# Attention rounds of a two-block transformer: all score products of a round at its head, in five banks, with the preceding pair's values behind them

## The chip, the cores and the metric

One Trainium2 chip, of which the program uses one core. The metric is device microseconds of one launch of the whole program, from inputs in HBM to the output in HBM. Engines are named as in the profile: PE is TensorE (the matrix engine), PEld its weight loads, DVE VectorE, ACT ScalarE, POOL GpSimd, SP the engine that issues most transfers. A bank is one of the eight PSUM banks of 128 x 512 f32, here G0, G1, S0, S1, T0, T1, O0 and O1 (bank0 to bank7).

## What is computed

Two transformer blocks on 512 tokens of width 1024, all in f32. The first has two kinds of attention, the second a gated linear attention and a dilated one:

```
block 1:  q,k,v of 8 MoBA heads (64 wide)  -> softmax(q k^T + bias) v        4 pairs of heads
          q1,q2,k1,k2,v of 4 diff heads    -> (softmax(q1 k1^T + bias)
                                             - lam * softmax(q2 k2^T + bias)) v, RMS norm   4 heads
          merged = sigmoid(ga) * (ya @ w_a) + sigmoid(gb) * (yb @ w_b);  x += norm(merged @ w_out)
          x += norm((silu(h @ w_gate) * (h @ w_up)) @ w_down)
block 2:  gated linear attention (4 heads) and dilated attention (8 heads = 4 pairs) side by side,
          then w_out, a causal convolution between w_up and the gating, w_down
```

All attention is causal. So of the 4 x 4 tiles of 128 queries by 128 keys, rows r = 0 to 3 have 1 to 4 tiles: 128, 256, 384 and 512 keys.

## The kernel before

Large products are made of f32r parts: each weight tile is split into w_hi and w_lo (ACT rounds, DVE subtracts, L1252 and L1833), each activation likewise, and one step is three matmuls of 128 x 512 (hi*hi, hi*lo, lo*hi). Everything inside attention (scores, transposes, values) is plain f32.

Attention goes in 12 rounds, i = 0 to 11, each with one pair: rounds 0 to 3 a pair of MoBA heads, 4 to 7 the two maps of one diff head, 8 to 11 a pair of dilated heads. All loops are unrolled, and each engine runs its own list in the order in which the code is written; semaphores are all that ties them. In a round PE has a filler, the projection or output steps of the next pair (32, 40 or 24 steps of three matmuls; `fill`, `dilated_fill`), and the attention work is put between the steps of the filler at the step numbers in the tables TURNS, LAST_TURNS (round 7) and DILATED_TURNS.

For pair i the work on PE is:

- `pair_scores(i, r)` (L858): for each of the two maps m, qT[64 rows of map m, 128 queries of row r] against k[64 rows, 128(r+1) keys]. Map 0 uses partitions 0 to 63 and bank S0, map 1 partitions 64 to 127 and bank S1: each is a 64 x 128 part of the array. In the trace one f32 matmul leaves two records.
- `turn(i, n)` (L877): transposes of the probabilities, n = 0 for rows 0 and 1, n = 1 for row 2, n = 2 for row 3, into banks T0 (map 0) and T1 (map 1; not used in rounds 4 to 7, where the maps have been joined).
- `pair_values(i)` (L895 and L898), a round later: values times transposed probabilities into O0. With two maps each is a 128 x 64 part of the array (L895), in rounds 4 to 7 it is the whole array (L898).
- `pair_squares` (L906) and, in the dilated rounds, `turn_dilated_values` (L1165) and `dilated_norm_sums` (L1172), which use bank O1.

In between, DVE reads the scores with the bias added (`pair_logits`, L1995, signals `sc_read`), ACT takes the exponential (`exps`, L1358), DVE and ACT scale by the row sum (`scale_rows` L2003 and L2007, `scale_other` L1366, `join_rows` L2017; signals `w_ready`, `w_other`), and after each turn DVE and ACT copy the transposed rows to SBUF (`store_turned`, L2027 to L2031, L1374 to L1378; signals `turned0`, `turned1`).

S0 and S1 hold rows 0 and 1 side by side, then row 2, then row 3, each written when the row before has been read. A round goes so on PE: scores of rows 0 and 1, filler, values of the preceding pair, scores of row 2, filler, turn 0, filler, scores of row 3, filler, turn 1, filler, turn 2, filler.

Of the kernel before, what the change touches and what calls it, by code (L numbers as in the profile page):

```python
# [26 lines left out]
P = 128  # L27
S = 512
# [64 lines left out]
TURNS = {4: (5, 9, 9, 13, 17, 23), 5: (5, 9, 9, 15, 21, 28)}  # L93
LAST_TURNS = (5, 9, 9, 12, 15, 20)
# [4 lines left out]
DILATED_TURNS = {24: (2, 5, 9, 11, 11, 15, 19, 20), 21: (1, 4, 8, 8, 9, 13, 13, 18)}  # L99
# [3 lines left out]
def two_maps(i):  # L103

    return i < 4 or i >= 8
# [79 lines left out]
def build(nc, a, out):  # L185
    with ExitStack() as ctx:
# [274 lines left out]
        def scores_at(r):  # L461

            return P if r == 1 else 0
# [153 lines left out]
        def _(pe):  # L617
# [230 lines left out]
            def pair_scores(i, r):  # L848

                n, at_ = P * (r + 1), scores_at(r)  # L850
                qk_ = qk if i < 8 else qk_dil
                for m in range(2):
                    if r == 0 and i >= 1:
                        pe.wait_ge(sc_read, 8 * i - 1 + m)
                    if r >= 2:
                        pe.wait_ge(sc_read, 8 * i + 2 * r - 1 + m)
                    h = slice(64 * m, 64 * m + 64)
                    ins = pe.matmul(SB_[m][:, at_:at_ + n], qk_[h, i % 2, 0, P * r:P * r + P], qk_[h, i % 2, 1, 0:n],  # L858
                                    start=True, stop=True)
                    if r >= 1:  # L860
                        ins.then_inc(sc_ready, 1)

            def turn(i, n):
# [4 lines left out]
                pe.wait_ge(w_ready, 4 * i + rows[-1] + 1)  # L868
                pe.wait_ge(turned0, 3 * i + n) if i or n else None
# [32 lines left out]
            def pair_squares(i):  # L902

                pe.wait_ge(o_sq, i - 3)
                pe.wait_ge(o_rs, i - 4) if i >= 5 else None
                pe.matmul(O1[:, :], ones[:, :], sqacc[:, :], start=True, stop=True).then_inc(o_ms, 1)  # L906

            for i in range(8):
                steps = KU * len(ROUNDS[i][1])
                values, scores2, turn0, scores3, turn1, turn2 = LAST_TURNS if i == 7 else TURNS[len(ROUNDS[i][1])]  # L910
# [18 lines left out]
                pair_scores(i, 3)  # L929
                fill(i, scores3, turn1)  # L930
# [229 lines left out]
            def turn_dilated_values(p):  # L1160

                pe.wait_ge(v_staged, p + 1)
                pe.wait_ge(qk_rs[1], p + 1)
                for j in range(NT):
# [1548 lines left out]
```

## Time and profile before

| | |
|---|---|
| median of 3 runs | 1394.62 us (1394.3 to 1395.87) |
| profiled execution, first to last instruction (span) | 1394.0 us |
| PE busy | 1375.2 us (99%), 6662 matmul records |
| PEld busy | 1105.7 us (79%) |
| DVE busy | 875.7 us (63%) |
| ACT busy | 584.4 us (42%) |
| rounds 0 to 7 | about 65 to 318 us of the span |
| rounds 8 to 11 | about 894 to 997 us |

The profiled execution has no time of its own beside its span; the three timed runs, which hold what lies before the first and after the last instruction, are 0.3 to 1.9 us above the span. A busy engine in this profile is one with an instruction under way. Records of matmuls overlap, since each lasts until its last result is written; how fast PE advances is read from the distance between the starts of matmuls.

### The profile page before, as it was taken

To read this page: it belongs to the slowest core of one execution; us is meant where nothing else is said; L and a number is where in the kernel's file an instruction comes from. 1 tells how busy PE (TensorE), PEld (TensorE's weight loads), DVE (VectorE), ACT (ScalarE), POOL (GpSimd) and SP (SyncE) were. 2 spreads that over 40 slices of the span, in tenths; PEclk is the share of its full clock that TensorE was granted. 3 is DMA by queue.
4 is the path that set the end of the run, shared out by engine and by line. 5 is a ranking of instruction groups with operands and counts; after the bars stand their busy time and mean duration, and the time that the engine had idled before them with its cause. 6 is when DMAs were issued, how large, how long until landed. Compare 5 with 4: busy or idle time off the path is not lost.

```text
span 1394.0 us, 18973 instructions
## 1 busy us (share of the span) xinstructions
PE 1375.2 (99%) x6662; PEld 1105.7 (79%) x6662; DVE 875.7 (63%) x1473; ACT 584.4 (42%) x979; POOL 57.4 (4%) x119
## 2 busy tenths in 40 slices
PE   9999999999999999999998999999999999999999
PEld 7777777778988888888885787777798888888887
DVE  6666666678777777774336777766566665665221
ACT  5444545553453323223224534666445444443221
POOL 0000000000001211211000000000000000000000
PEclk9999999999999999999999999999999999999999
DMA  5222122213225555554431221111212322223332
GB/s 205 92 75 76 67 70 76 76 61 121 91 73 190 197 190 190 192 194 153 141 124 47 96 68 61 62 61 62 72 61 92 104 90 101 94 93 116 93 98 87
DMA packets 42614, 146.82 MB, mean 105 GB/s; under 512 B 5424, under 2 KB 5696, under 8 KB 42560
## 3 DMA queue, kind: packets, MB, share of 16 engines
q1 hardware_dynamic: 34592, 120.13, 26.1%
q0 software_dynamic: 7824, 25.70, 5.4%
q8 instruction: 35, 0.57, 0.2%
q10 hardware_dynamic: 144, 0.26, 0.1%
q14 instruction: 19, 0.16, 0.0%
HBM read 143.97 MB, written 2.10 MB: 105 GB/s over the span
## 4 chain that ended last, share of the span: by engine, by line
PE 93%; DVE 4%; ACT 2%; issue 1%; DMA 0%; SPq 0%; DVEq 0%; ACTq 0%
PE bank L634 62%; PE bank L836 13%; PE bank L652 4%; PE bank L775 3%; PE bank L858 2%; PE bank L877 2%; PE bank L950 2%; PE bank L895 1%; PE bank L742 1%; PE bank L1080 1%; PE bank L898 1%; DVE w_lo L1833 1%; DVE gate_a L2040 0%; DVE hbuf L1893 0%; PE bank L1172 0%
## 5 line engine op out<-in xcount | busy, mean ns | idle before, releaser
L1833 DVE TENSOR_TENSOR w_lo<-raw,w_hi 128x1024 fp32r<-128x1024 f32 (+1 forms) x224 | 268.0, 1197 | 160.8 <-ACT w_hi L1252 155.9
L1252 ACT ACTIVATE w_hi<-raw 128x1024 fp32r<-128x1024 f32 (+1 forms) x224 | 231.6, 1035 | 285.9 <-PE bank L634 260.7
L634 PE MATMUL bank<-h_hi,w_hi 128*128 128x512 f32 x856 | 339.5, 397 | 0.7 <-DVE w_lo L1830 0.5
L634 PE MATMUL bank<-h_hi,w_lo 128*128 128x512 f32 x856 | 334.1, 390 | 0.0
L634 PE MATMUL bank<-h_lo,w_hi 128*128 128x512 f32 x856 | 334.0, 390 | 0.0
L634 PEld LDWEIGHTS bank<-h_hi,w_hi 128*128 128x128 f32 x856 | 161.0, 188 | 41.2 <-issue 7.4
L634 PEld LDWEIGHTS bank<-h_hi,w_lo 128*128 128x128 f32 x856 | 161.1, 188 | 33.9
L634 PEld LDWEIGHTS bank<-h_lo,w_hi 128*128 128x128 f32 x856 | 161.1, 188 | 33.3 <-issue 1.0
L634 PE MATMUL bank<-f_hi,w_lo 128*128 128x512 f32 x352 | 136.9, 389 | 0.0
L634 PE MATMUL bank<-f_hi,w_hi 128*128 128x512 f32 x352 | 136.9, 389 | 0.0
L634 PE MATMUL bank<-f_lo,w_hi 128*128 128x512 f32 x352 | 136.9, 389 | 0.0
L836 PE MATMUL bank<-h_hi,w_hi 128*128 128x512 f32 x240 | 98.4, 410 | 0.4 <-DVE ma L2046 0.4
L836 PE MATMUL bank<-h_hi,w_lo 128*128 128x512 f32 x240 | 93.9, 391 | 0.0
L836 PE MATMUL bank<-h_lo,w_hi 128*128 128x512 f32 x240 | 93.6, 390 | 0.0
L634 PEld LDWEIGHTS bank<-f_hi,w_hi 128*128 128x128 f32 x352 | 66.1, 188 | 13.8
L634 PEld LDWEIGHTS bank<-f_hi,w_lo 128*128 128x128 f32 x352 | 66.1, 188 | 13.6
L634 PEld LDWEIGHTS bank<-f_lo,w_hi 128*128 128x128 f32 x352 | 66.1, 188 | 13.6
L2258 DVE CUSTOM_DVE_ANT_0 ada<-ada,cond 128x512 f32<-128x512 f32 x96 | 63.5, 689 | 16.5 <-DMA ada<-in_w_ada 15.0
L520 POOL DMA_DIRECT2D ada<-in_w_ada x96 | 51.5, 536 | 364.8 <-DVE ada_sum L2258 358.8
L836 PEld LDWEIGHTS bank<-h_hi,w_hi 128*128 128x128 f32 x240 | 45.1, 188 | 21.4 <-issue 13.6
L2244 DVE TENSOR_TENSOR f_lo<-fbuf,f_hi 128x512 f32 (+1 forms) x44 | 30.5, 692 | 43.0 <-ACT f_hi L1794 21.5
L836 PEld LDWEIGHTS bank<-h_hi,w_lo 128*128 128x128 f32 x240 | 45.0, 188 | 10.1
(351 smaller groups left out, 1954.3 us busy)
## 6 DMA issues: line engine op xcount, KB each, us to landing
raw<-in_w_up SPq DMA_DIRECT2D x66, 512.0 KB, 3.3
ada<-in_w_ada POOLq DMA_DIRECT2D x96, 256.0 KB, 3.1
raw<-in_w_mix SPq DMA_DIRECT2D x47, 512.0 KB, 3.3
raw<-in_w_down SPq DMA_DIRECT2D x32, 512.0 KB, 3.5
raw<-in_w_in SPq DMA_DIRECT2D x25, 512.0 KB, 3.3
raw<-in_w_gate SPq DMA_DIRECT2D x22, 512.0 KB, 3.2
raw<-in_w_out SPq DMA_DIRECT2D x16, 512.0 KB, 3.3
raw<-in_w_down SPq DMA_DIRECT2D x16, 384.0 KB, 3.3
```

Source lines behind the costliest of these rows:

```text
L520: pool.dma_start(ada[:, half, :], a["w_ada"][bass.ds(t, 1), :, half * S:half * S + S] .rearrange("t p k -> (t p) k")).then_inc(ada_in[half ...
L634: last = pe.matmul(to[:, :], wt[:, slot, k, :], act_[:, rhs0 + k, :], start=(k == first and n == 0), stop=(k == K - 1 and n == 2))
L652: last = pe.matmul(to[:, TOKENS[h]], wt[:, slot, k, :], act_[:, k, TOKENS[h]], start=(k == 0 and m == 0), stop=(k == KU - 1 and m == 2))
L775: last = pe.matmul(banks[r][:, :], xt[:, k, P * r:P * r + P], wt[:, slot, 4 * kk:4 * kk + 4, :].rearrange("p a b -> p (a b)"), start=(k == ...
L836: last = pe.matmul(output_bank(u)[:, :], wt[:, slot, k, :], act_[:, kr, :], start=(kr == 0 and m == 0), stop=(kr == length - 1 and m == 2))
L858: ins = pe.matmul(SB_[m][:, at_:at_ + n], qk_[h, i % 2, 0, P * r:P * r + P], qk_[h, i % 2, 1, 0:n], start=True, stop=True)
L877: last = pe.transpose(TB[m][:, at_:at_ + P], probs_[:, m, ROWOFF[r] + P * j:ROWOFF[r] + P * j + P], ident[:, :])
L950: last = pe.matmul(output_bank(u)[:, :], wt[:, slot, 4 * half + k, :], act_[:, 4 + k, :], start=(k == 0 and m == 0), stop=(k == 3 and m == 2))
L1252: act.activation(w_hi[:, s, k0:K, :], raw[:, s, k0:K, :], ACT.Copy).then_inc(hi_ready[s], 1)
L1833: dve.tensor_tensor(w_lo[:, s, k0:K, :], raw[:, s, k0:K, :], w_hi[:, s, k0:K, :].bitcast(F32), ALU.subtract).then_inc(split_ready[s], 1)
L2244: dve.tensor_tensor(at_k(f_lo, j), fbuf[:, :], at_k(f_hi, j).bitcast(F32), ALU.subtract).then_inc(f_ready, 1)
L2258: dve.tensor_tensor_reduce(ada[:, half, :], ada[:, half, :], cond[:, half * S:half * S + S], 1.0, 0.0, ALU.mult, ALU.add, ada_sum[:, parit ...
```

## The change

- `pair_scores(i)` now issues all eight matmuls of the pair at the head of the round, in the order SCORES (map, row): (0,0), (1,0), (0,2), (1,2), (0,1), (1,3), (0,3), (1,1). They go to five banks: row 3 to S0 and S1, rows 0 and 2 side by side to T0 (map 0) and T1 (map 1), row 1 of both maps side by side to O1. Before (1,1) it waits until (0,1) is done, which is in the same bank. Five of the matmuls signal instead of six.
- `pair_values(i - 1)` follows straight behind, before the first filler step.
- Ahead of the scores are new waits: all turned rows of the preceding pair stored, all its scores read; in rounds 6 and 7 O1 read by the norm; in round 8 `gy_f32`, which was ahead of turn 0. Turn 0, the squares and the turned dilated values wait for the reads of T0, T1 and O1.
- DVE reads the rows in the order 0, 2, 1, 3, the first three at the head of the round. Row 3 keeps its place.
- The tables lose the entries for scores and values. The turned dilated values go from step 2 to 4 (in round 11 from 1 to 3); all turns, squares and norm sums keep their step numbers.

```diff
-TURNS = {4: (5, 9, 9, 13, 17, 23), 5: (5, 9, 9, 15, 21, 28)}
-LAST_TURNS = (5, 9, 9, 12, 15, 20)
+TURNS = {4: (9, 9, 17, 23), 5: (9, 9, 21, 28)}
+LAST_TURNS = (9, 9, 15, 20)
+SCORES = ((0, 0), (1, 0), (0, 2), (1, 2), (0, 1), (1, 3), (0, 3), (1, 1))
+SCORED = ((0, 2), (1, 2), (0, 1), (0, 3), (1, 1))
+READABLE = {(0, 0): 1, (0, 2): 1, (1, 0): 2, (1, 2): 2, (0, 1): 5, (1, 1): 5, (0, 3): 5, (1, 3): 5}
+READ_ORDER = (0, 2, 1, 3)
-DILATED_TURNS = {24: (2, 5, 9, 11, 11, 15, 19, 20), 21: (1, 4, 8, 8, 9, 13, 13, 18)}
+DILATED_TURNS = {24: (4, 9, 11, 15, 19, 20), 21: (3, 8, 8, 13, 13, 18)}
...
-        def scores_at(r):
-
-            return P if r == 1 else 0
+        def scores_of(m, r):
+
+            if r == 3:
+                return SB_[m][:, :]
+            if r == 1:
+                return O1[:, 2 * P * m:2 * P * m + 2 * P]
+            return TB[m][:, 0:P] if r == 0 else TB[m][:, P:S]
...
+            def pair_scores(i):
+
                 qk_ = qk if i < 8 else qk_dil
...
+                if i >= 1:
+                    pe.wait_ge(turned0, 3 * i)
+                    pe.wait_ge(sc_read, 8 * i)
+                    if two_maps(i - 1):
+                        pe.wait_ge(turned1, turned_other(i - 1, 3))
+                if i in (6, 7):
+                    pe.wait_ge(o_rs, i - 5)
+                for m, r in SCORES:
+                    n, h = P * (r + 1), slice(64 * m, 64 * m + 64)
+                    if (m, r) == (1, 1):
+                        pe.wait_ge(sc_ready, 5 * i + SCORED.index((0, 1)) + 1)
+                    ins = pe.matmul(scores_of(m, r), qk_[h, i % 2, 0, P * r:P * r + P], qk_[h, i % 2, 1, 0:n],
                                     start=True, stop=True)
-                    if r >= 1:
+                    if (m, r) in SCORED:
                         ins.then_inc(sc_ready, 1)
...
+                if n == 0:
+                    pe.wait_ge(sc_read, 8 * i + 4)
...
-                pair_scores(i, 0)
-                pair_scores(i, 1)
-                fill(i, 0, values)
+                pair_scores(i)
                 if i >= 1:
                     pair_values(i - 1)
-                pair_scores(i, 2)
-                fill(i, values, scores2)
+                fill(i, 0, squares)
                 if i >= 5:
                     pair_squares(i - 1)
-                fill(i, scores2, turn0)
+                fill(i, squares, turn0)
                 turn(i, 0)
-                fill(i, turn0, scores3)
-                pair_scores(i, 3)
-                fill(i, scores3, turn1)
+                fill(i, turn0, turn1)
                 turn(i, 1)
...
-                pair_logits(i, 0)
-                pair_logits(i, 1)
+                for r in READ_ORDER[0:3]:
+                    pair_logits(i, r)
                 split_lo((first + 2) % SLOTS)
...
-                pair_logits(i, 2)
                 split_lo((first + 3) % SLOTS)
                 scale_rows(i, 2)
```

How the instructions stand on PE at the head of round 1, before (L858 are scores, L895 values, L836 filler; `x2` is one for each map, `...` is filler left out):

```order
L836 MATMUL bank<-h_hi,w_lo 128x512
L858 MATMUL bank<-qk 128x128 x2
L858 MATMUL bank<-qk 128x256 x2
L836 MATMUL bank<-h_hi,w_hi 128x512
...
L836 MATMUL bank<-h_hi,w_lo 128x512
L895 MATMUL bank<-pT_moba,v_moba 64x512 x2
L895 MATMUL bank<-pT_moba,v_moba 64x384 x2
L895 MATMUL bank<-pT_moba,v_moba 64x256 x2
L895 MATMUL bank<-pT_moba,v_moba 64x128 x2
L858 MATMUL bank<-qk 128x384 x2
L836 MATMUL bank<-h_hi,w_hi 128x512
```

Twelve filler steps later stands the pair of 128x512 scores, by itself between fillers. The same place in the changed kernel (L872 are scores, L911 values, L846 filler):

```order
L846 MATMUL bank<-h_hi,w_lo 128x512
L872 MATMUL bank<-qk 128x128 x2
L872 MATMUL bank<-qk 128x384 x2
L872 MATMUL bank<-qk 128x256
L872 MATMUL bank<-qk 128x512 x2
L872 MATMUL bank<-qk 128x256
L911 MATMUL bank<-pT_moba,v_moba 64x512 x2
L911 MATMUL bank<-pT_moba,v_moba 64x384 x2
L911 MATMUL bank<-pT_moba,v_moba 64x256 x2
L911 MATMUL bank<-pT_moba,v_moba 64x128 x2
L846 MATMUL bank<-h_hi,w_hi 128x512
```

Three separate places of scores and one of values have become one run; the last four scores are no longer in pairs of one width.

On DVE the head of round 1 before (L1995 reads scores; the `negmaxs` rows fetch the row maxima):

```order
L1995 ISA probs,negmaxs<-bank,dist_52,cols 128x128
L1995 ISA negmaxs 128x1
...
L1995 ISA probs,negmaxs<-bank,dist_52,cols 128x256
L1995 ISA negmaxs 128x1
...
L1833 TENSOR_TENSOR w_lo<-raw,w_hi 128x1024
L2003 RECIPROCAL rrows<-rowsums 128x2
L2007 TENSOR_SCALAR probs<-probs,rrows 128x128
```

and in the changed kernel (L2003 reads scores; each read is there once for each map in both lists):

```order
L2003 ISA probs,negmaxs<-bank,dist_52,cols 128x128
L2003 ISA negmaxs 128x1
...
L2003 ISA probs,negmaxs<-bank,dist_52,cols 128x384
L2003 ISA negmaxs 128x1
...
L2003 ISA probs,negmaxs<-bank,dist_52,cols 128x256
L2003 ISA negmaxs 128x1
...
L1841 TENSOR_TENSOR w_lo<-raw,w_hi 128x1024
L2011 RECIPROCAL rrows<-rowsums 128x2
L2015 TENSOR_SCALAR probs<-probs,rrows 128x128
```

The two reads of row 2 have moved ahead of those of row 1, and ahead of the splitting of a weight tile and the scaling of rows 0 and 1.

## Rows read from the trace of the kernel before

**Rows 1.** page, parts 1, 2 and 4: busy times, clock, chain

```profile
PE 1375.2 (99%) x6662; PEld 1105.7 (79%) x6662; DVE 875.7 (63%) x1473; ACT 584.4 (42%) x979; POOL 57.4 (4%) x119
...
PEclk9999999999999999999999999999999999999999
...
PE 93%; DVE 4%; ACT 2%; issue 1%; DMA 0%; SPq 0%; DVEq 0%; ACTq 0%
```

**Rows 2.** groups by shape, PE: busy us, mean ns | idle before

```profile
L858 PE MATMUL bank<-qk 64*128 64x512 f32 x32 | 9.0, 641 | 0.0
...
L858 PE MATMUL bank<-qk 64*128 64x384 f32 x32 | 7.3, 535 | 0.0
```

**Rows 3.** chain of waits, filler of round 0: start us, us, what

```profile
86.43 6.13 PE bank L836 x27
```

**Rows 4.** timeline, PE, first scores of round 1: start us, us, instruction

```profile
92.17 0.39 PE L836 MATMUL bank<-h_hi,w_lo 128*128 128x512 f32 x1
92.49 0.93 PE L858 MATMUL bank<-qk 64*128 64x128 f32 x8
...
93.69 0.39 PE L836 MATMUL bank<-h_lo,w_hi 128*128 128x512 f32 x1
```

**Rows 5.** timeline, PE, values and row 2 in round 1

```profile
96.66 0.39 PE L836 MATMUL bank<-h_hi,w_lo 128*128 128x512 f32 x1
96.98 2.37 PE L895 MATMUL bank<-pT_moba,v_moba 128*64 128x512 f32 x16
99.28 0.92 PE L858 MATMUL bank<-qk 64*128 64x384 f32 x4
...
100.47 0.40 PE L836 MATMUL bank<-h_lo,w_hi 128*128 128x512 f32 x1
```

**Rows 6.** timeline, PE, row 3 in round 1

```profile
106.15 0.39 PE L836 MATMUL bank<-h_hi,w_lo 128*128 128x512 f32 x1
106.47 1.13 PE L858 MATMUL bank<-qk 64*128 64x512 f32 x4
...
107.86 0.39 PE L836 MATMUL bank<-h_lo,w_hi 128*128 128x512 f32 x1
```

**Rows 7.** timeline, PE, last values of round 11, between fillers

```profile
993.40 0.39 PE L634 MATMUL bank<-y_hi,w_lo 128*128 128x512 f32 x1
...
996.36 0.40 PE L634 MATMUL bank<-y_lo,w_hi 128*128 128x512 f32 x1
```

**Rows 8.** timeline, PE, values and row 2 in round 5 (whole array)

```profile
220.52 0.39 PE L836 MATMUL bank<-h_hi,w_lo 128*128 128x512 f32 x1
...
224.18 0.39 PE L836 MATMUL bank<-h_lo,w_hi 128*128 128x512 f32 x1
```

**Rows 9.** timeline, PE, first filler step of round 5

```profile
217.23 0.47 PE L836 MATMUL bank<-h_hi,w_hi 128*128 128x512 f32 x1 [0.20 <-DVE ma L2046]
```

**Rows 10.** timeline, DVE, round 8: row 1 scaled, row 2 read

```profile
900.89 0.35 DVE L2007 TENSOR_SCALAR probs_dil<-probs_dil,rrows 128x256 f32<-128x256 f32 x1
...
901.76 0.61 DVE L1995 CUSTOM_DVE_ANT_0 probs_dil<-bank,dist_dil,cols 128x384 f32<-128x384 f32 x1
```

**Rows 11.** timeline, ACT and PE, round 8: rows 0 and 1 scaled; turn 0

```profile
900.49 0.90 ACT L1366 ACTIVATE probs_dil<-probs_dil,rrows 128x128 f32<-128x128 f32 x2 [1.37 <-DVE rrows L2003]
...
902.64 0.82 PE L877 MATMUL bank<-ident,probs_dil 128*128 128x128 f32 x6
```

**Rows 12.** timeline, DVE and PE: end of round 8, head of 9

```profile
916.79 0.68 DVE L2031 COPY pT_dil<-bank 128x512 f32<-128x512 f32 x1
...
918.56 0.93 PE L858 MATMUL bank<-qk_dil 64*128 64x128 f32 x8
```

**Rows 13.** timeline, DVE and PE: last gyf, head of round 8

```profile
892.45 0.69 DVE L2468 TENSOR_TENSOR gyf<-bank,gres 128x512 f32<-128x512 f32 x1
...
893.96 0.93 PE L858 MATMUL bank<-qk_dil 64*128 64x128 f32 x8
```

**Rows 14.** timeline, PE, turn 2 of round 7

```profile
302.68 0.66 PE L877 MATMUL bank<-ident,probs 128*128 128x128 f32 x4 [0.89 <-DVE probs L2017]
```

More of the change, by code:

```diff
@@ L846, in fill @@
                     step(i, n)
-            def pair_scores(i, r):
-                n, at_ = P * (r + 1), scores_at(r)
+            def pair_scores(i):
                 qk_ = qk if i < 8 else qk_dil
[L852 to L858, printed above, removed]
+                if i >= 1:
[10 more added lines that the diff above has]
+                    ins = pe.matmul(scores_of(m, r), qk_[h, i % 2, 0, P * r:P * r + P], qk_[h, i % 2, 1, 0:n],
                                     start=True, stop=True)
-                    if r >= 1:
+                    if (m, r) in SCORED:
                         ins.then_inc(sc_ready, 1)
@@ L905, in pair_squares @@
                 pe.wait_ge(o_rs, i - 4) if i >= 5 else None
+                pe.wait_ge(sc_read, 8 * min(i + 1, 7) + 6)
                 pe.matmul(O1[:, :], ones[:, :], sqacc[:, :], start=True, stop=True).then_inc(o_ms, 1)
@@ L909, in _ @@
                 steps = KU * len(ROUNDS[i][1])
-                values, scores2, turn0, scores3, turn1, turn2 = LAST_TURNS if i == 7 else TURNS[len(ROUNDS[i][1])]
+                squares, turn0, turn1, turn2 = LAST_TURNS if i == 7 else TURNS[len(ROUNDS[i][1])]
                 if i == 0:
@@ L1163, in turn_dilated_values @@
                 pe.wait_ge(qk_rs[1], p + 1)
+                pe.wait_ge(sc_read, 8 * (p + 8) + 6)
                 for j in range(NT):
@@ L1175, in _ @@
                 steps = 24 if i < 11 else 21
-                turned, values, turn0, norm_q, scores3, turn1, norm_k, turn2 = DILATED_TURNS[steps]
+                turned, turn0, norm_q, turn1, norm_k, turn2 = DILATED_TURNS[steps]
                 p = i - 8
@@ L1179, in _ @@
                 pe.wait_ge(k_taken, p + 1)
-                pair_scores(i, 0)
-                pair_scores(i, 1)
+                if i == 8:
+                    pe.wait_ge(gy_f32, w.next(gy_f32, times=2))
+                pair_scores(i)
+                if i > 8:
+                    pair_values(i - 1)
                 dilated_fill(i, 0, turned)
                 turn_dilated_values(p)
-                dilated_fill(i, turned, values)
-                if i > 8:
-                    pair_values(i - 1)
-                pair_scores(i, 2)
-                dilated_fill(i, values, turn0)
-                if i == 8:
-                    pe.wait_ge(gy_f32, w.next(gy_f32, times=2))
+                dilated_fill(i, turned, turn0)
                 turn(i, 0)
@@ L1983, in pair_logits @@
             def pair_logits(i, r):
-                n, at_, p = P * (r + 1), scores_at(r), ROWOFF[r]
+                n, p = P * (r + 1), ROWOFF[r]
                 probs_ = probs if i < 8 else probs_dil
@@ L1989, in pair_logits @@
                 for m in range(2):
-                    dve.wait_ge(sc_ready, 6 * i + (1 if r <= 1 else 2 * r - 1) + m)
+                    dve.wait_ge(sc_ready, 5 * i + READABLE[m, r])
                     if i >= 1:
@@ L2518, in _ @@
                 p = i - 8
-                pair_logits(i, 0)
-                pair_logits(i, 1)
+                for r in READ_ORDER[0:3]:
+                    pair_logits(i, r)
                 split_lo(2)
```

9 lines of the change are left out of this document (3 added, 6 removed).

## The prediction

> **What bounds the kernel now.** I read the page first: PE is busy for 99% of the span, at full granted clock in all 40 slices, and 93% of the chain that ended last is PE [rows 1]. So what counts is the time that PE's list takes, and that an instruction is "busy" does not say that it is of use. The question is where PE's list has time in it that is not columns. For that I took the starts of matmuls from the timeline around each kind of attention work, and compared them with the columns that pass.
>
> Two rates are needed. A filler matmul (512 columns) takes 6.13 / 27 = 0.227 us [rows 3]. A record of a score matmul of 512 columns lasts 641 ns, one of 384 columns 535 ns [rows 2]: 106 ns for 128 columns, whatever a record's fixed part is. One f32 matmul leaves two records, so 128 columns cost 0.212 us, a whole map of scores (1280 columns) 2.12 us, and a pair's values the same. Maps 0 and 1 run side by side: the four records of row 2, each with 0.32 us of columns, lie in 0.92 us [rows 5]; in series their columns alone would need 1.27.
>
> Now the blocks, from the last filler before to the second filler after, less two filler matmuls (0.454) and less the columns:
> - scores of rows 0 and 1: 93.69 - 92.17 = 1.52 us; less 0.454 and 0.64 leaves 0.43 [rows 4].
> - values and row 2: 100.47 - 96.66 = 3.81; less 0.454 and 2.12 + 0.64 leaves 0.60 [rows 5].
> - row 3: 107.86 - 106.15 = 1.71; less 0.454 and 0.85 leaves 0.41 [rows 6].
> - values alone (end of round 11): 996.36 - 993.40 = 2.96; less 0.454 and 2.12 leaves 0.39 [rows 7].
> - values on the whole array with row 2 (round 5): 3.66; less 0.454 and 2.76 leaves 0.45 [rows 8].
>
> So what costs is not the work but each passage between a divided array (64 x 128 for scores, 128 x 64 for values) and the whole one: about 0.41 for going in and out once, whatever is inside. Whole-array values cost next to nothing themselves (0.45 against 0.43). And values next to scores cost 0.60, not 0.39 + 0.41 = 0.80: one passage of about 0.2 is saved.
>
> **The change part by part.**
>
> Removed passages. A two-map round pays 0.43 + 0.60 + 0.41 = 1.44 before. After it pays one block of scores with values behind: 0.60 again, if scores to values costs as much as values to scores did. Saved: 0.84. Round 0 has no values: 0.43 + 0.42 + 0.41 becomes 0.43, saved 0.83; round 8 likewise. Rounds 5 to 7: 0.43 + 0.45 + 0.41 becomes 0.45, saved 0.84. All twelve rounds: 12 x 0.84 = 10.1 us. The columns are the same before and after.
>
> The passage from 64 x 128 to 128 x 64 is in no row. It lies between nothing (both count as one divided array) and twice the 0.2 of the other direction; I take 0.2, the nearest row. It occurs in seven rounds (1 to 4 and 9 to 11), so the bounds are 1.5 us to either side. Row 5 shows that 128 x 64 to 64 x 128 was not free. The Trainium skill says in "TensorEngine Tiling (Array Packing)", Key Properties, that a change of the tiling mode, unlike one of the tile, drains the engine. By that rule the new passage costs a drain as the old one did and the sum stays; without it the sum would be 1.5 us better. The trace agrees with the rule on every passage that it has.
>
> A wait that goes. In rounds 5 and 6 the first filler step finds its output bank still unread by DVE: 0.20 us idle in round 5 [rows 9], and the same in round 6. In the new order 4.3 us of scores and values (2.12 + 2.12 and passages) stand ahead of that step, so the wait is over before. Saved: 0.4 us.
>
> Unequal pairs. The last four score matmuls are 256 beside 512 and 512 beside 256 columns. If each map's part goes on by itself, both end after 1280 columns. The wait ahead of (1,1) is for (0,1): its columns end after 768 of map 0, 1.27 us into the block, and the record's part beyond its columns (535 - 318 = 0.22 us) makes 1.49; map 1 reaches (1,1) after 1024 columns, 1.70. The spare time is 0.2 us, so I cost the wait at nothing; each 0.1 us by which the signal came later than that would cost 1.2 us in all.
>
> New waits at the head of a round. In the two-map rounds the turned rows must be stored; the tightest is in the dilated part, where DVE's store of row 3 ends at 916.79 + 0.68 = 917.47 and scores start at 918.56 [rows 12]: 1.1 us to spare. What follows turn 1 up to there keeps its step numbers, so the distance stays. In round 8 the last `gyf` ends at 893.14, scores start at 893.96 [rows 13]: 0.8 us to spare. Both at nothing. If one were late, all of PE's queue would stand behind it, one for one.
>
> DVE. The reads of row 2 (two of about 0.54, the distance of starts in 0.61 us records, [rows 10]) now delay the weights of rows 0 and 1 by 1.1 us. Turn 0 is at the same step, and comes 0.85 - 0.4 us later than before, since all of row 3 is ahead of it and half of the saving. The tightest place is round 8, where DVE starts late: ACT ended row 1 at 900.49 + 0.90 = 901.39, turn 0 began at 902.64 [rows 11]. Spare 1.25 + 0.45 - 1.1 = 0.6 us. Cost nothing. For turns 1 and 2 DVE gains: in round 8 it reads row 2 at 901.76 now [rows 10], and would do so at the round's head.
>
> Round 7. PE waits there before turn 2, 0.89 us, for DVE's joined row 3 [rows 14]. That chain hangs on the output that PE finishes at step 8, which now comes 0.4 us later for the scores ahead of it; but DVE no longer has row 2's reads in it (1.1 us). I leave this wait as it is, so that the round saves its 0.84 only as far as the chain moves too: about 0.7. The 0.1 is within rounding.
>
> Sum: 10.1 + 0.4 = 10.5 us. The profiled span of 1394.0 becomes 1383.5; the median is 0.6 above the span, so 1394.6 - 10.5 = 1384.1 us.
>
> **The rivals.**
>
> Pace of the longer. If a matmul on one map can't start before the partner of the one before has ended, the unequal pairs cost 512 + 512 columns where 768 pass: 256 x 1.66 ns = 0.43 us a round, 5.1 in all: 1389.2. Against it: nothing in the trace starts in step except what is of equal width; for it: the trace has no unequal pair at all.
>
> DVE falls behind. The weights for turn 0, or row 3 in rounds 6 and 7, come later than PE. Each such round gives back up to its 0.84. For it: DVE is 63% busy over the span [rows 1], and one turn waits for it already [rows 14]. Against: the spare times above. With four of twelve rounds given back: 10.5 - 3.4, 1387.5.
>
> Slower: no overlap. Place: the four unequal matmuls. If they ran one after another (other widths, and row 1 of both maps in one bank O1, which never occurred before), they would take 1536 columns, 2.55 us, instead of 1.27: 1.28 a round, 15.4 in all, against 10.5 saved: 1399.5. It decides from 0.87 us a round. The equal pairs that overlap in the trace speak against it [rows 5]. The Trainium skill ("TensorEngine Tiling (Array Packing)", Restrictions and Gotchas, Gotcha 1) says that row tiles cannot use one bank at the same time. By that rule the two maps' row 1 in O1 must come one after the other, which the wait before (1,1) ensures and which costs only what that wait does; no row here has two maps in one bank of scores.
>
> No effect. The passages are only where PE's waiting shows, and other engines set the pace of the rounds. Then 1394.6 stays. Against: PE is idle for only 1394.0 - 1375.2 = 18.8 us of the whole span [rows 1], and none of the blocks above names a releaser [rows 4 to 8].
>
> **How the numbers follow.** Forecast 0.72 (its own range 1382.6 to 1385.6, the two bounds of the unseen passage); pace of the longer 0.07; DVE behind 0.11; no effect 0.04; slower 0.06. The range 1382.6 to 1388.0 holds the forecast and most of "DVE behind". A difference of under 0.2% (2.8 us) is about what a measurement of this kernel cannot tell from none. Faster by more: forecast, longer pace and DVE behind, 0.90; within: 0.04; slower: 0.06.
>
> **What would show it.** After the change PE has twelve blocks of 16 score records in place of 36 shorter ones, and in all rounds but 0 and 8 the values stand right behind. From the last filler before to the second filler after it should be 0.454 + 2.12 + 2.12 + 0.60 = 5.3 us in two-map rounds, 5.15 in rounds 5 to 7, and 3.0 in rounds 0 and 8. A block 0.4 longer speaks for the pace of the longer, 1.3 longer for no overlap. The distance from the head of round 9 to that of round 10 should be 0.8 shorter than before. Round 5 should have no idle time at its first filler step; turn 0 in round 8 should have no releaser. I am wrong if the score blocks are as short as that and the turns wait, or if filler elsewhere has grown.

## The result

The changed kernel takes 1384.4 us (median of 4 runs, 1383.96 to 1385.69) where the kernel before took 1395.2 in the same series (4 runs, 1394.3 to 1395.87). The ratio is 0.9922, 95% interval 0.991 to 0.9933. A second series of 5 runs gave 1384.4 again, ratio 0.9925 (0.9911 to 0.9939). The forecast was 1384.1. The single times of each kernel gather at two levels, about 1394.4 and 1396.0 us before and 1384.2 and 1385.8 after, so that a median moves by up to 1.6 us with the number of runs on each level, while like levels differ by about 10.2 us.

The page of the changed kernel's profile, to be read against [rows 1] (busy times and numbers of records):

```profile
PE 1364.7 (99%) x6662; PEld 1113.0 (81%) x6662; DVE 873.8 (63%) x1473; ACT 584.9 (42%) x979; POOL 57.4 (4%) x119
```

The span is 1382.6 us. PE has the same 6662 matmul records, and is busy for 10.5 us less; DVE and ACT are where they were. The page alone says no more, so we go to the blocks. Round 1 on PE's timeline (start us, us, line and instruction), from the last filler matmul before the block to the second one after it, answers to [rows 4 to 6]:

```profile
91.72 0.39 PE L846 MATMUL bank<-h_hi,w_lo 128*128 128x512 f32 x1
92.04 2.43 PE L872 MATMUL bank<-qk 64*128 64x128 f32 x16
94.40 2.37 PE L911 MATMUL bank<-pT_moba,v_moba 128*64 128x512 f32 x16
...
97.04 0.40 PE L846 MATMUL bank<-h_lo,w_hi 128*128 128x512 f32 x1
```

97.04 - 91.72 = 5.32 us, and from the starts in ns 5.319 in every two-map round. Less two fillers (0.454) and 2.12 + 2.12 of columns leaves 0.62. The prediction had 0.60, and [rows 4 to 6] together had 1.44 (1.43 from the starts in ns). The 16 records of scores stand in one row, so nothing came between them.

The starts in ns also show where a passage spends its time. The first score record starts 319 ns behind the last filler, where fillers follow one another at 227: 0.09 us. The next record of the same map follows at 213 ns, where 128 columns take 107: another 0.11. The second part goes with the weights (PEld). A filler's are loaded well ahead of it, here at 91.50 for the product at 91.72; the first scores' only as their product starts, at 92.04:

```profile
91.50 0.19 PEld L846 LDWEIGHTS bank<-h_hi,w_lo 128*128 128x128 f32 x1
92.04 2.03 PEld L872 LDWEIGHTS bank<-qk 64*128 64x128 f32 x16 [0.35 <-issue]
```

The same two parts stand at the passage from scores to values (0.09 and 0.05 us) and from values to filler (0.10 and 0.11); the rest of the 0.62 lies in hundredths between the records. That the late weights are the reason for the second part is inferred from these rows; runs 2 and 5 below show the same 0.10 us at a product whose weights come late for another reason.

Round 5, whose values use the whole array, against [rows 8]:

```profile
211.84 0.39 PE L846 MATMUL bank<-y_hi,w_lo 128*128 128x512 f32 x1
212.16 2.43 PE L872 MATMUL bank<-qk 64*128 64x128 f32 x16
...
216.70 0.48 PE L846 MATMUL bank<-h_hi,w_hi 128*128 128x512 f32 x1
217.01 0.39 PE L846 MATMUL bank<-h_lo,w_hi 128*128 128x512 f32 x1
```

5.17 us (5.175 from the starts in ns), leftover 0.48 (predicted 0.45), and the row of the first filler step names no releaser any more, where [rows 9] had 0.20 us behind DVE's `ma`. Round 8, scores alone:

```profile
885.24 0.39 PE L644 MATMUL bank<-h_hi,w_lo 128*128 128x512 f32 x1
885.56 2.43 PE L872 MATMUL bank<-qk_dil 64*128 64x128 f32 x16
...
888.25 0.39 PE L644 MATMUL bank<-h_lo,w_hi 128*128 128x512 f32 x1
```

3.01 us (predicted 3.0), leftover 0.44. PE's waits at the head of round 0 (0.78 us) and behind the last values of round 11 (0.53 us) are in both kernels alike. Two others stand in the timeline of the changed kernel's rounds. The first is the old one before turn 2 of round 7 [rows 14], a little longer; the second is new, in round 8, before the column sums of the next pair's squared keys:

```profile
295.83 0.66 PE L893 MATMUL bank<-ident,probs 128*128 128x128 f32 x4 [1.04 <-DVE probs L2025]
...
903.54 0.39 PE L644 MATMUL bank<-h_hi,w_lo 128*128 128x512 f32 x1
904.10 1.13 PE L1185 MATMUL bank<-qk_sq,blk 128*128 128x512 f32 x2 [0.16 <-ACT next_k L1500]
```

The bracket of the second counts only 0.16 us, but the matmul starts 0.56 us behind the filler before it; where nothing is waited for that step is 0.23. From the starts in ns the place costs 0.42 us more than in rounds 9 and 10 (1.745 us from the filler before to the second one after, against 1.328).

**How much of it is the change.** The distance between the starts of two rounds' first score matmuls doesn't depend on where the kernel's start lies. In us, with the second profile of each kernel in brackets where it differs by over 0.03:

| from to | before | after | shorter by |
|---|---|---|---|
| round 0 to 1 | 27.50 | 26.66 | 0.84 |
| 1 to 2, 2 to 3, 3 to 4, each | 29.80 | 28.93 | 0.87 |
| 4 to 5 | 34.21 | 33.34 | 0.87 |
| 5 to 6 | 35.13 (35.09) | 34.01 | 1.12 (1.09) |
| 6 to 7 | 29.69 | 28.65 (28.69) | 1.04 (1.00) |
| 7 to the next stage | 55.27 | 54.54 | 0.73 |
| from there to round 8 | 557.77 (556.30) | 556.20 (556.28) | 1.57 (0.02) |
| 8 to 9 | 24.60 (24.56) | 23.93 | 0.67 (0.65) |
| 9 to 10, 10 to 11, each | 26.55 | 25.80 | 0.75 |
| 11 to the start of PE's last matmul | 418.72 | 417.94 | 0.79 |

The rounds give 0.84 + 4 x 0.87 + 1.12 + 1.04 + 0.73 + 0.67 + 2 x 0.75 + 0.79 = 10.2 us, and 10.0 with the second profiles. The 1.57 between round 7's end and round 8 is not the change's: it is gone in the second pair of profiles (below).

### The profile page after: what moved, and what is told of

It reads as the page before. It is cut to its first block, busy times and chain, and to the rows that moved or that the text cites. A ratio compares the mean times of both kernels' runs of the same rounds, so it can differ in the third digit from the quotient of the medians.

```text
span 1382.6 us, 18985 instructions
## 1 busy us (share of the span) xinstructions
PE 1364.7 (99%) x6662; PEld 1113.0 (81%) x6662; DVE 873.8 (63%) x1473; ACT 584.9 (42%) x979; POOL 57.4 (4%) x119
## 4 chain that ended last, share of the span: by engine, by line
PE 92%; DVE 4%; ACT 3%; issue 1%; DMA 0%; DVEq 0%; SPq 0%; ACTq 0%
PE bank L644 61%; PE bank L846 13%; PE bank L662 4%; PE bank L785 3%; PE bank L872 2%; PE bank L962 2%; PE bank L893 1%; PE bank L911 1%; PE bank L752 1%; PE bank L1092 1%; PE bank L914 1%; DVE w_lo L1841 0%; DVE hbuf L1901 0%; ACT w_hi L1260 0%; DVE xT L2197 0%
## 5 line engine op out<-in xcount | busy, mean ns | idle before, releaser
L846 PE MATMUL bank<-h_hi,w_hi 128*128 128x512 f32 x240 | 96.4, 402 | 0.0
L846 PE MATMUL bank<-h_hi,w_lo 128*128 128x512 f32 x240 | 93.7, 390 | 0.0
L846 PE MATMUL bank<-h_lo,w_hi 128*128 128x512 f32 x240 | 93.6, 390 | 0.0
L846 PEld LDWEIGHTS bank<-h_hi,w_lo 128*128 128x128 f32 x240 | 45.1, 188 | 9.7
L846 PEld LDWEIGHTS bank<-h_hi,w_hi 128*128 128x128 f32 x240 | 45.1, 188 | 9.4 <-issue 1.0
```

The lines of the kernel that those rows point to most:

```text
L846: last = pe.matmul(output_bank(u)[:, :], wt[:, slot, k, :], act_[:, kr, :], start=(kr == 0 and m == 0), stop=(kr == length - 1 and m == 2))
```

## The experiments

All are built on the changed kernel unless said otherwise. Single products are named (map, row). The distances are read as in the table above; the medians scatter by 1.5 us and more, so with differences this small the trace decides and the median is its check. Theory: a passage between the divided and the whole array costs, about 0.4 us for in and out; what is done inside costs its columns only. The rivals are that the leftover belongs to interruptions of the filler, to the products, or to the unequal widths, and that the gain came from waits.

**1. Values back to a step of their own**

```diff
                 pair_scores(i)
+                fill(i, 0, 5)
                 if i >= 1:
                     pair_values(i - 1)
-                fill(i, 0, squares)
+                fill(i, 5, squares)
```

(in the dilated rounds one step behind the turned values, the same way)

> All scores at the head of the round as in the changed kernel (1384.4 us), but the values of the preceding pair go back to a step of their own (step 5). Theory (a passage between the divided and the whole array costs, the work inside does not): in the seven rounds with 64-wide values the one block with 0.60 us over its columns becomes two with 0.43 and 0.39, so +0.2 us each, and in rounds 5 to 7, where the values use the whole array, nothing: +1.4 us, 1385.8. Rival (each interruption of the filler costs about 0.4 us, whatever it holds): ten rounds more with a second interruption, +4 us, 1388.4.

Measured: 1388.2 us (5 runs, 1386.3 to 1389.8), ratio to before 0.9953 (0.9939 to 0.9966); profiled span 1386.5. Round 1, scores and values:

```profile
92.09 0.39 PE L846 MATMUL bank<-h_hi,w_lo 128*128 128x512 f32 x1
92.41 2.43 PE L872 MATMUL bank<-qk 64*128 64x128 f32 x16
...
95.11 0.39 PE L846 MATMUL bank<-h_lo,w_hi 128*128 128x512 f32 x1
...
98.09 0.39 PE L846 MATMUL bank<-h_hi,w_lo 128*128 128x512 f32 x1
98.41 2.37 PE L911 MATMUL bank<-pT_moba,v_moba 128*64 128x512 f32 x16
...
101.05 0.40 PE L846 MATMUL bank<-h_lo,w_hi 128*128 128x512 f32 x1
```

3.02 and 2.96 us (3.012 and 2.960 in ns): leftovers of 0.44 and 0.39 in place of one of 0.62. Rounds with 64-wide values are 0.24 us longer (0.21 in rounds 9 and 10, 0.33 in round 11), rounds 5 to 7 only 0.04 or 0.05. That is the theory's picture: the rival wanted 0.4 in rounds 5 to 7 too. The values of round 5, now by themselves between fillers:

```profile
219.17 0.39 PE L846 MATMUL bank<-h_hi,w_lo 128*128 128x512 f32 x1
219.40 2.32 PE L914 MATMUL bank<-pT_diff,v_diff 128*128 128x512 f32 x8
...
221.79 0.39 PE L846 MATMUL bank<-h_lo,w_hi 128*128 128x512 f32 x1
```

2.62 us, only 0.04 over two fillers and 2.12 of columns. These are plain f32 products between f32r fillers, as the scores are, but on the whole array. So neither the interruption nor the change of the number format makes the leftover: the division of the array does. All rounds together are 1.8 us longer (1.4 expected). The median is 3.8 longer and by itself would speak for the rival; the profiled execution shows what else is in it: 1.6 us more between round 7 and round 8, where nothing was changed (a dip of the clock, below), and 0.4 at the start.

**2. Row 3 of the scores back to its own step**

```diff
-SCORES = ((0, 0), (1, 0), (0, 2), (1, 2), (0, 1), (1, 3), (0, 3), (1, 1))
+SCORES = ((0, 0), (1, 0), (0, 1), (1, 2), (0, 2), (1, 1), (0, 3), (1, 3))
...
+                fill(i, turn0, scores3)
+                score_matmuls(i, SCORES[6:8])
-                fill(i, turn0, turn1)
+                fill(i, scores3, turn1)
```

(the first six at the head; `sc_ready` and what waits for it counted anew)

> Row 3 of the scores goes back to its own step between turn 0 and turn 1 in all twelve rounds (the order of the rest is changed so that row 1 of the two maps still does not meet in its bank); everything else as changed (1384.4). Theory: one passage in and out more in every round, 12 x 0.41 = +4.9 us, 1389.3; the head block's 0.60 (0.43, 0.45) stays. Rival (the gain came from the values standing behind the scores, or from waits that went, not from row 3): +0 to 1 us.

Measured: 1391.8 us (9 runs, 1390.4 to 1392.2), ratio 0.9972 (0.9963 to 0.9982). Head and row 3 of round 1:

```profile
93.86 0.39 PE L846 MATMUL bank<-h_hi,w_lo 128*128 128x512 f32 x1
94.18 1.67 PE L877 MATMUL bank<-qk 64*128 64x128 f32 x12
...
98.43 0.40 PE L846 MATMUL bank<-h_lo,w_hi 128*128 128x512 f32 x1
...
107.55 0.39 PE L846 MATMUL bank<-h_hi,w_lo 128*128 128x512 f32 x1
107.87 1.13 PE L877 MATMUL bank<-qk 64*128 64x512 f32 x4
...
109.26 0.39 PE L846 MATMUL bank<-h_lo,w_hi 128*128 128x512 f32 x1
```

Row 3's own block costs 1.71 us, 0.41 over its columns, the passage to the hundredth. The head should be the changed kernel's 5.32 less 0.85 for row 3's columns, 4.47 us, and is 4.57: 0.10 more. In the new order (0,1) ends after 384 columns of map 0 and (1,1) comes after 512 of map 1, 128 columns apart where the changed kernel has 256. The starts in ns show what that does. The weights of (1,1), which wait for (0,1), are loaded 56 ns behind the end of its record in both kernels. In the changed kernel that is 217 ns ahead of the product, here 4 ns. The product itself is not late (980 ns into the block, as (1,3) is in the changed kernel with 979), but its first record lasts 478 ns instead of 376 and the second follows at 318 ns instead of 216. It shows in the mean of the four 256-column records of a round, first the changed kernel, then this one (busy us, mean ns | idle before):

```profile
L872 PE MATMUL bank<-qk 64*128 64x256 f32 x32 | 9.5, 376 | 0.0
```

```profile
L877 PE MATMUL bank<-qk 64*128 64x256 f32 x32 | 10.3, 401 | 0.0
```

4 x 25 = 100 ns. So the blocks of one round are 0.51 us longer, not 0.41, and the distance of the rounds is 0.59 longer. The rule holds for row 3 and the rival falls (0 to 1 us); the expected total was too low (4.9, against 6.2 in the rounds and 7.4 by the medians), because the new order had a price of its own.

**3 and 4. One more pair of products, inside the block or apart**

```diff
# 3
+                for m in range(2):
+                    pe.matmul(scores_of(m, 0), ...)      # (0,0) and (1,0) once more
                 for m, r in SCORES:
# 4: the same, and behind it
+                fill(i, 0, 1)
...
-                fill(i, 0, squares)
+                fill(i, 1, squares)
```

> The two score products of row 0 are made twice, the second time right behind the first, inside the block. Theory: only their columns, 0.21 us a round (the two maps side by side), 12 x 0.21 = +2.5 us, 1386.9. Rival (every score product costs something beyond its columns, so that the leftover grows with the number of products): 0.1 us a pair more, +3.7 us, 1388.1.

> The same extra pair of row 0, but one filler step ahead of the block, so that the array is divided once more in each round. Theory: 0.21 us of columns and 0.43 for going in and out, 12 x 0.64 = +7.7 us, 1392.1; the difference to the run with the pair inside is 12 x 0.43 = 5.1 us. Rival (the leftover belongs to the products): the same as inside, 1386.9.

Measured: inside 1388.7 us (4 runs, 1386.8 to 1389.8), apart 1395.2 (10 runs, 1393.8 to 1398.4), ratios 0.9953 (0.9938 to 0.9968) and 1.0002 (0.9992 to 1.0011). First the run with the pair inside (the 16 score records and the values left out), then with the pair apart, round 1 (L870 is the extra pair):

```profile
93.60 0.39 PE L846 MATMUL bank<-h_hi,w_lo 128*128 128x512 f32 x1
93.92 0.49 PE L870 MATMUL bank<-qk 64*128 64x128 f32 x4
...
99.14 0.40 PE L846 MATMUL bank<-h_lo,w_hi 128*128 128x512 f32 x1
```

```profile
92.31 0.39 PE L846 MATMUL bank<-h_hi,w_lo 128*128 128x512 f32 x1
92.62 0.49 PE L870 MATMUL bank<-qk 64*128 64x128 f32 x4
...
93.38 0.39 PE L846 MATMUL bank<-h_lo,w_hi 128*128 128x512 f32 x1
```

Inside: 5.54 us against 5.32, 0.22 for 0.212 us of columns, and 0.25 in the distance of the rounds, which lies between the 0.21 of the theory and the 0.31 of the rival; the block, where the rival has its price, speaks for the theory. All rounds are 2.8 us longer (2.5 expected); another 1.7 stand ahead of round 0, where this run's clock dips (below). Apart: 93.38 - 92.31 = 1.07 us, less 0.454 and 0.21 leaves 0.41, and 0.63 in the distance of the rounds (0.64 expected). It is the same work on the same data, and only the filler step between makes the difference, 0.39 us a round. This pair of runs is the most direct evidence for the theory, and it says that even the smallest piece of divided work pays the full passage.

Run 4 shows a second thing, in rounds 5 and 6, which are 1.3 us longer and not 0.63, so that all rounds together are 9.6 longer (7.7 expected; 0.5 of it is in round 11 and was not followed up):

```profile
216.40 0.47 PE L846 MATMUL bank<-h_hi,w_hi 128*128 128x512 f32 x1 [0.63 <-DVE ma L2058]
```

With only the extra pair ahead of the first filler step, that step again finds its bank unread, as in [rows 9]; with 4.7 us ahead of it, it does not. So the 0.2 us that rounds 5 and 6 gained beyond the rest came from there.

**5. Pairs of equal width**

```diff
-SCORES = ((0, 0), (1, 0), (0, 2), (1, 2), (0, 1), (1, 3), (0, 3), (1, 1))
+SCORES = ((0, 0), (1, 0), (0, 2), (1, 2), (0, 3), (1, 3), (0, 1), (1, 1))
```

> The scores in pairs of equal width: rows 0, 2, 3, 1, so that (1,1) waits for (0,1), its neighbour in the bank, with nothing of its own in between. Theory (each half of the array runs at its own pace, unequal pairs cost nothing): nothing is gained by equal widths, and the wait now costs (0,1) and its signal, about 0.65 us a round in place of 0.42 beside it (one f32 product of 256 columns: 0.42 of columns and 0.22 to the end of its last record, then (1,1) alone with 0.42, where 0.42 were needed for both): 12 x 0.65 = +7.8 us, 1392.2. Rival (pace of the longer: the unequal pairs of the changed kernel cost 0.43 a round): 0.65 - 0.43 = 0.22 a round, +2.6 us, 1387.0. Rival (row 1 in one bank is harmless to time, the signal comes early): 0.

Measured: 1393.1 us (10 runs, 1392.6 to 1394.5), ratio 0.9979 (0.997 to 0.9989). The block of round 1:

```profile
93.81 0.39 PE L846 MATMUL bank<-h_hi,w_lo 128*128 128x512 f32 x1
94.12 3.18 PE L872 MATMUL bank<-qk 64*128 64x128 f32 x16
...
99.87 0.40 PE L846 MATMUL bank<-h_lo,w_hi 128*128 128x512 f32 x1
```

The 16 score records take 3.18 us in place of 2.43: 0.75 a round, near the 0.65 that the theory gave and far from the 0.22 of "pace of the longer". From the starts in ns (1,1) begins 57 ns behind the end of (0,1)'s last record, 0.643 us later in the block than in the changed kernel, which is the expected 0.64; its weights are loaded 2 ns ahead of it, and its first record takes 480 ns instead of 376. 0.643 + 0.104 = 0.747: what the expectation left out is the weight load, as in run 2. So the order (0,1), (1,3), (0,3), (1,1) of the change costs nothing for its unequal widths and is what hides the wait between the two products that share a bank. Without it, 8.5 of the change's 10.2 us (the sum over the rounds) would be gone; round 8 is only 0.31 us longer, since its wait for the staged keys is then over in time.

**6. Rows read in order 1, 2, 3, 4**

```diff
-READ_ORDER = (0, 2, 1, 3)
+READ_ORDER = (0, 1, 2, 3)
...
-                    pe.wait_ge(sc_read, 8 * i + 4)
+                    pe.wait_ge(sc_read, 8 * i + 6)
```

> VectorE reads the rows in order 1, 2, 3, 4 instead of 1, 3, 2, 4. Row 2 can be read only at the block's end, so that the third row's two reads of 0.54 us come 1.1 us later than in the changed kernel. Theory (passages on PE set the time, VectorE has room): nothing in ten rounds; in round 8, where turn 0 has under 1 us to spare, up to 0.4 us; together 0 to +0.5 us, 1384.4 to 1384.9. Rival (VectorE sets the pace in round 7, where PE waits 1.0 us for it already): +1.1 us there and 0.4 in round 8, 1385.9.

Measured: 1384.2 us (4 runs, 1384.0 to 1385.3), ratio 0.9914 (0.9899 to 0.9929). All rounds are as in the changed kernel to 0.04 us but round 8, which is 0.44 us shorter: the direction that neither the theory nor the rival had. The cause is on ACT. The changed kernel first, then this one, round 8, DVE's first reads and what ACT does behind them:

```profile
885.56 2.43 PE L872 MATMUL bank<-qk_dil 64*128 64x128 f32 x16
...
887.50 0.35 DVE L2003 CUSTOM_DVE_ANT_0 probs_dil<-bank,dist_dil,cols 128x128 f32<-128x128 f32 x1
...
889.64 0.51 ACT L1366 ACTIVATE probs_dil<-probs_dil,negmaxs 128x256 f32<-128x256 f32 x1 [0.87 <-DVE negmaxs L2003]
...
890.64 1.04 ACT L1260 ACTIVATE w_hi<-raw 128x1024 fp32r<-128x1024 f32 x1
891.72 1.23 DVE L1841 TENSOR_TENSOR w_lo<-raw,w_hi 128x1024 fp32r<-128x1024 f32 x1 [1.71 <-ACT w_hi L1260]
```

```profile
886.94 2.43 PE L872 MATMUL bank<-qk_dil 64*128 64x128 f32 x16
...
888.91 0.34 DVE L2003 CUSTOM_DVE_ANT_0 probs_dil<-bank,dist_dil,cols 128x128 f32<-128x128 f32 x1
...
891.16 1.05 ACT L1260 ACTIVATE w_hi<-raw 128x1024 fp32r<-128x1024 f32 x1
892.24 1.23 DVE L1841 TENSOR_TENSOR w_lo<-raw,w_hi 128x1024 fp32r<-128x1024 f32 x1 [0.64 <-ACT w_hi L1260]
```

DVE starts its reads equally late in both (1.94 and 1.97 us behind the first score product). ACT's exponentials go by rows 0, 1, and then a weight conversion; with row 2 read in between, ACT stands idle for 0.87 us before row 1, the conversion starts 5.08 us behind the first product instead of 4.22, and DVE, which needs it, waits 1.71 us instead of 0.64. All of ACT's list behind it moves by that, down to `next_k`, for which PE waits in round 8. In the rounds where DVE comes in time the order changes nothing, since row 1 is complete only at the block's end.

**7. Values ahead of the scores**

```diff
-                pair_scores(i)
                 if i >= 1:
                     pair_values(i - 1)
+                pair_scores(i)
```

> The preceding pair's values stand ahead of the round's scores instead of behind them: 128x64 then 64x128, the direction that the kernel before had. Theory (both directions cost the same, about 0.2 us): blocks of 0.60 over their columns as in the changed kernel, no difference on PE; but scores come 2.1 us later, which VectorE may not make up before turn 0: in round 8 nothing (it has no values), in rounds 1 to 7 and 9 to 11 turn 0 may wait. So blocks 4.87 us long, and 0 to +2 us in waits at turn 0: 1384.4 to 1386.4. Rival (the direction matters): blocks 0.2 us shorter or longer in seven rounds.

Measured: 1387.8 us (4 runs, 1387.3 to 1388.9), ratio 0.9943 (0.9927 to 0.9958). The block of round 1 runs from 91.41 (the filler before) to 96.73: 5.32 us, and from the starts in ns it is 4.865 us beyond two fillers, as in the changed kernel. The direction of the passage between the two divisions makes no difference. What costs is what hangs on the scores: turn 2 of round 7 waits longer, and a filler step of round 11 that needs pair 10's output waits:

```profile
91.41 0.39 PE L846 MATMUL bank<-h_hi,w_lo 128*128 128x512 f32 x1
...
96.73 0.40 PE L846 MATMUL bank<-h_lo,w_hi 128*128 128x512 f32 x1
...
296.08 0.66 PE L893 MATMUL bank<-ident,probs 128*128 128x128 f32 x4 [1.60 <-DVE probs L2025]
...
973.28 0.50 PE L644 MATMUL bank<-y_hi,w_hi 128*128 128x512 f32 x1 [1.80 <-DVE y_lo L2066]
```

1.60 - 1.04 + 1.80 = 2.4 us, and 0.29 each in rounds 9 and 10 at the squared keys; 3.2 in all rounds, more than the 0 to 2 expected. The wait at turn 0 that was expected did not come.

**8 and 9. The two waits moved, and both orders together**

```diff
-LAST_TURNS = (9, 9, 15, 20)
+LAST_TURNS = (9, 9, 15, 22)
...
-                    fill(i, turn2, 22)
+                    fill(i, turn2, 24)
                     pair_values(7)
-                    fill(i, 22, 25)
+                    fill(i, 24, 27)
...
                 turned, turn0, norm_q, turn1, norm_k, turn2 = DILATED_TURNS[steps]
+                norm_k += i == 8
```

(9 has the edit of 6 as well)

> The changed kernel with the two places moved at which PE still waits: in round 7 turn 2 from step 20 to 22 (values from 22 to 24, squares from 25 to 27), in round 8 the squares of the keys from step 19 to 20. Theory: the waits of 1.0 us (for the joined row 3) and 0.4 us (for the staged keys) go and nothing else turns late: -1.4 us, 1383.0. Rival (the waits move: the values of pair 7 come too late for the output products behind round 7, or turn 2 of round 8 waits in place of the squares): within 0.3 us of 1384.4.

> The version with the two waits moved, and VectorE's reads in the order 1, 2, 3, 4 as well. In order, round 8 was 0.44 us shorter than the changed kernel, since ScalarE's second exponential and the weight conversion behind it start 0.75 us earlier there; moving the squares of the keys by one step brought 0.51. Theory (both cure the same wait, the squares of the keys that wait for the staged keys): no sum of the two, the rounds as in the version with the waits moved to 0.1 us, time equal within 0.1%, about 1382.7 us. Rival (separate gains): 0.4 us less again.

Measured: 1384.0 us (5 runs, 1383.2 to 1386.2), ratio 0.9917 (0.9904 to 0.9931), and 1383.9 (5 runs, 1382.4 to 1384.3), ratio 0.9915 (0.9901 to 0.9928), beside 1384.4 (ratio 0.9925) for the changed kernel in the latter's series. The same two places in run 9 name no releaser. By the distances round 7 is 1.23 us shorter than in the changed kernel and round 8 0.51, in both runs: 1.7 us, a little more than the 1.4 expected; nothing else turned late. Run 9 has no further gain, so 6 and 8 cure the same wait. (The expectation's 0.75 us for the earlier start on ACT is 0.86 by the rows of run 6.) The profiled span of run 9 is 1380.8 us against 1382.4 of the changed kernel. The intervals of the ratios overlap, so by the medians this gain is not shown; the distances show it, from one profile of each run.

**10 and 11. Both kernels once more**

> The kernel before once more, for a second profile. In its first profile the granted clock falls to 0.68 for 4 us in the gated-attention stage (864 to 868 us), 110 us ahead of round 8, and that stretch is 1.5 us longer than in the changed kernel, whose instructions there are the same. Theory (the dip comes and goes with the run and is not of the change): this profile has no dip there, 113.4 us from that stage's first product to round 8, and a span some 1.4 us shorter, about 1392.6; the rounds keep their lengths to 0.05 us. Rival (the order of the rounds before brings the dip): it is there again, 114.9 us.

> The changed kernel once more, on the same chip as the version with both waits moved. Theory: 1384.4 us again, ratio 0.992 to the kernel before, the rounds equal to 0.05 us to those of its first profile; the stretch from the start to round 0 may differ by up to 2 us from run to run.

Measured: before 1394.4 us (one run, span 1392.7); after 1384.4 (5 runs, 1384.1 to 1386.0), ratio 0.9925 (0.9911 to 0.9939), span 1382.4. Busy time and granted clock by stretch (the columns after the window: its length, PE, PEld, DVE, ACT, POOL busy with counts, PEclk, DMA share, GB/s) in the gated-attention stage, first profile of the kernel before, then its second:

```profile
864.00:868.00 4.00, 3.69 (x15) 3.10 (x16) 3.81 (x6) 2.17 (x2) 0.00 (x0) 0.68 0.39 130
```

```profile
864.00:868.00 4.00, 3.45 (x22) 3.09 (x23) 3.85 (x5) 2.40 (x2) 0.00 (x0) 1.00 0.37 104
```

In both, PE has stood still for 2.0 us before it (until 864.31 and 864.55 us), and in the changed kernel likewise (until 857.43). Behind that, one of the two is granted 0.68 of the full clock on average, that is, part of the stretch at the lower of the two levels, 1.2 instead of 2.4 GHz: 15 matmuls where otherwise 22 pass, and 1.4 us more up to round 8 (114.9 against 113.5 from that stage's first product). So the dip is not made by the change, as far as so few profiles can say: the kernel before has it in one profile of two, the changed kernel in none of two, and of the nine experiments on the changed kernel the first has it, the others do not. The comparison of the two profiles without it is 1392.7 - 1382.4 = 10.3 us, 0.2 of that ahead of round 0.

## Why the prediction was right

**The rule.** The step on which all rested, that passages cost and the work inside does not, held in every form in which it was asked: 0.62, 0.48 and 0.44 us of leftover in the three kinds of blocks [rows 4 to 8 gave 0.60, 0.45, 0.43], 0.41 for row 3 or for one extra pair alone, 0.39 for values alone. Removed per round: 0.84 predicted, 0.87 measured in rounds 1 to 4, 0.84 in round 0, 0.75 in rounds 9 and 10. The blocks themselves give 0.80, in round 1 as in round 9. The rest is in the filler between the blocks, which the window from filler to filler didn't count: it takes 0.07 us less in rounds 1 to 4 and 0.05 more in rounds 9 and 10. Why it does so in the dilated rounds stays open.

**The unseen passage** from 64 x 128 to 128 x 64 was taken at 0.2 us, with 0 and 0.4 as bounds. A block of a two-map round lasts 5.319 us. Beyond values alone (2.960) and 2.12 of columns that is 0.24, beyond scores alone (3.012) 0.19. Run 7 gives the same with the order reversed. By the rule in the Trainium skill's "TensorEngine Tiling (Array Packing)", Key Properties, that a change of the tiling mode drains the engine, neither direction should be free, and neither is.

**Unequal pairs and the shared bank.** The block is not 0.43 nor 1.28 us longer, so neither "pace of the longer" nor "no overlap" holds. From the starts in ns, (0,3) begins 1.404 us into the block, when (1,3) is half through (its second record starts at 1.408), so each map goes on by itself. The wait before (1,1) shows nothing, but it had less to spare than the sum's 0.2 us: that sum left out 56 ns up to the weight load and the load's own time. The weights come 217 ns ahead of (1,1), and where they come only with the product it costs 0.10, so about 0.1 us was to spare (an estimate from runs 2 and 5). Where the spare time is taken away it shows, 0.10 us in run 2 and 0.75 in run 5. In "TensorEngine Tiling (Array Packing)", Restrictions and Gotchas, Gotcha 1, the Trainium skill says that row tiles cannot use one bank at the same time; no run here let them, since all of them wait.

**The waits that go.** 0.4 us was predicted for rounds 5 and 6; they are 1.12 and 1.04 shorter where rounds 1 to 4 are 0.87: 0.42. Run 4 brings the wait back.

**Round 7.** 0.7 predicted, 0.73 measured. The wait became 1.04 us from 0.89, so DVE's chain came earlier by less than PE did. Run 2, whose head is shorter by row 3, has no wait there at all. That fits a chain that starts from PE's progress at the head, but the chain was not tested by itself.

**DVE and the new waits at a round's head.** Turn 0 of round 8 has no releaser, and no head of a round waits but round 0's, as before. But the step looked only at turn 0. The delay of row 1 behind row 2's reads went through ACT's queue instead (run 6) and came out at the squared keys in round 8, 0.42 us. The same round lost an old wait of 0.29 us, also not in the prediction, so that it is 0.65 to 0.67 shorter where 0.84 was expected. This is the one step of the mechanism that was wrong, by 0.4 us: of the reads that were moved I followed DVE's list to the next turn, not ACT's behind it.

**The sum.** Predicted 10.5 us; the rounds gave 10.0 to 10.2, and like levels of the run times about 10.2. The medians of the first series differ by 10.8, since they fall differently between the two levels. That 1384.1 is within 0.3 us of the measured 1384.4 is partly luck. The prediction took the median 0.6 us above the span, from a profile with the dip and a median of other runs; a profiled execution takes 1.7 us more than its own span (1384.31 against 1382.6, 1394.39 against 1392.7). The span it started from, 1394.0, is in turn 1.3 us longer than that of the second profile (1392.7). The two errors, 1.1 too little and 1.3 too much, nearly cancel, and what is left of them is offset in part by the gain that was 0.3 to 0.5 us too large. "No effect" and "DVE behind" are out: no turn but the one in round 7 waits.

## What to carry to other kernels

Divided and whole use of the array should be grouped: here each in-and-out costs 0.4 us in f32 whatever is inside, so the number of borders counts, and a small piece of divided work is best put next to another. Two products that must share a bank one after the other want a longer product of another bank between them on the second one's half, long enough that the signal and the second one's weight load (56 ns and 0.10 us here) are over before its turn comes; unequal widths on the two halves cost nothing. When a reader's order is changed, follow the queue of every engine that waits for it to its end: here the price of a read moved by 1 us came out on PE 15 us later, by way of ACT.

## What was not expected of the hardware

- The granted clock can dip in some executions and not in others, at the same place of the same program: 0.68 for 4 us, worth 1.4 us, in 2 of 13 profiles. PE stands still for 2.0 us just before that place in all 13. Over the first 20 us it is 0.91 in two others (runs 2 and 3), whose round 0 starts 1.7 us later than the changed kernel's; in runs 5 and 6 it starts 1.4 and 1.3 us later with no such dip, so that the start wavers for other reasons too. A third dip, between 740 and 760 us, where PE stands still for 4.3 us, is in all 13 profiles and differs in length: the granted clock over these 20 us is 0.83 in the first profile of the changed kernel and 0.91 in its second, yet the stretch up to round 8 lasts the same (556.20 and 556.28 us). Whether the dip behind 864 us is what sets the two levels of the run times apart is not shown, since only the profiled executions have a trace.
- A block's length repeats to 1 or 2 ns over rounds and runs, so that an effect of 0.1 us can be read from one trace of this kernel where the medians, 1 us and more apart from run to run, don't resolve it.
